# Where four pieces of bookkeeping stand in a two-block transformer kernel: two output projections' first weight pieces, a feed-forward norm, a key-value norm

## The reference

```python
def second_block(x, ...):
    for l in range(2):
        h = rmsnorm(x, g_attn[l])
        if l < 1: x = x + dsa_mixer(h, ...)           # sparse attention, then o @ w_o
        else:     x = x + nsa_mixer(h, kv_shared, ...) # three-branch attention, then o @ w_o
        x = x + sq_relu_mlp(rmsnorm(x, g_mlp[l]), w_up[l], w_down[l])
        if l == 0: kv_shared = shared_kv(x, ...)       # rmsnorm(x, g_kv) @ w_kv, then compressed blocks
    return rmsnorm(x, g_final)

def sq_relu_mlp(h, w_up, w_down):                      # 1024 -> 4096 -> 1024
    return jnp.square(jax.nn.relu(h @ w_up)) @ w_down
```

## Time and profile before

| | |
|---|---|
| median of 3 runs | 2052.91 us (2050.9 to 2053.53) |
| the profiled execution's own time | 2053.22 us |
| its span, first to last instruction | 2051.5 us |
| PE busy | 1959.5 us, 96% of the span, 9117 matmuls |
| DVE busy | 986.1 us, 48% |
| ACT busy | 662.8 us, 32% |
| POOL busy | 158.6 us, 8% |
| share of the chain that ended last | PE 86%, DVE 7%, ACT 2%, DMA 2% |
| mean granted PE clock | 0.978 of full speed |

### The profile page before, as it was taken

The page is one execution under the profiler, slowest core; times in us unless marked ns, Lnnn a source line. Parts: engine busy times, 40 slices in busy tenths (PEclk is TensorE's granted clock), DMA queues, the critical chain, the costliest instruction groups (busy, mean ns, idle before and its releaser), DMA issues.

```text
span 2051.5 us, 23968 instructions
## 1 busy us (share of the span) xinstructions
PE 1959.5 (96%) x9117; PEld 1357.6 (66%) x9117; DVE 986.1 (48%) x1865; ACT 662.8 (32%) x1238; POOL 158.6 (8%) x169
## 2 busy tenths in 40 slices
PE   7999899987999999988999999999999999999998
PEld 3478577573333334445788888878777778888886
DVE  6473645342121222674465455545256756455554
ACT  2572721141011112367332222232336633222222
POOL 1000000021111110213200000010000020000001
PEclk9999999997999999999999999999999999999999
DMA  9545143457999786111222322322540022232211
GB/s 323 196 125 205 43 160 128 186 175 280 417 381 354 274 338 226 42 42 42 83 82 82 122 84 82 123 82 82 172 153 2 1 83 82 82 124 82 83 40 41
DMA packets 104871, 292.55 MB, mean 143 GB/s; under 512 B 13445, under 2 KB 24403, under 8 KB 91712
## 3 DMA queue, kind: packets, MB, share of 16 engines
q1 hardware_dynamic: 92352, 266.60, 35.3%
q0 software_dynamic: 11408, 22.27, 3.5%
q10 hardware_dynamic: 1008, 2.29, 0.3%
HBM read 331.22 MB, written 24.69 MB: 173 GB/s over the span
## 4 chain that ended last, share of the span: by engine, by line
PE 86%; DVE 7%; ACT 2%; DMA 2%; issue 1%; POOL 1%; ACTq 0%; DVEq 0%; SPq 0%; POOLq 0%
PE bank L1402 17%; PE bank L1404 17%; PE bank L1403 17%; PE bank L1798 8%; PE bank L1319 5%; PE bank L1824 4%; PE bank L1361 3%; PE bank L1387 2%; PE bank L1373 2%; PE bank L1854 1%; PE bank L1606 1%; PE bank L1782 1%; DVE top L3268 1%; PE bank L1393 1%; DVE hT L3269 1%
## 5 line engine op out<-in xcount | busy, mean ns | idle before, releaser
L3159 DVE TENSOR_TENSOR weights_low<-weight_ring,weights_high 128x1024 fp32r<-128x1024 f32 x128 | 161.2, 1260 | 269.6 <-ACT weights_high L2282 269.6
L1404 PE MATMUL bank<-hidden_high,weights_low 128*128 128x512 f32 x704 | 274.5, 390 | 0.0
L1402 PE MATMUL bank<-hidden_high,weights_high 128*128 128x512 f32 x640 | 249.7, 390 | 6.0 <-DVE weights_low L2748 3.8
L1403 PE MATMUL bank<-hidden_low,weights_high 128*128 128x512 f32 x640 | 249.7, 390 | 0.0
L2282 ACT ACTIVATE weights_high<-weight_ring 128x1024 fp32r<-128x1024 f32 x128 | 135.6, 1060 | 324.2 <-PE bank L1404 324.2
L1402 PE MATMUL bank<-normed_high,weights_high 128*128 128x512 f32 x512 | 201.5, 394 | 3.9 <-DVE weights_low L3159 3.9
L1404 PE MATMUL bank<-normed_high,weights_low 128*128 128x512 f32 x512 | 200.6, 392 | 0.0
L1403 PE MATMUL bank<-normed_low,weights_high 128*128 128x512 f32 x512 | 200.5, 392 | 0.0
L1798 PE MATMUL bank<-weight_ring,arena 128*64 128x512 f32 x464 | 173.7, 604 | 4.4 <-issue 2.5
L1404 PEld LDWEIGHTS bank<-hidden_high,weights_low 128*128 128x128 f32 x704 | 132.6, 188 | 27.6
L1402 PEld LDWEIGHTS bank<-hidden_high,weights_high 128*128 128x128 f32 x640 | 120.5, 188 | 32.1 <-DVE weights_low L2748 7.0
(11 more groups left out here) (551 smaller groups left out, 3493.2 us busy)
## 6 DMA issues: line engine op xcount, KB each, us to landing
weight_ring<-in_w_up SPq DMA_DIRECT2D x16, 2048.0 KB, 8.7
weight_ring<-in_w_down SPq DMA_DIRECT2D x16, 2048.0 KB, 7.8
weight_ring<-in_w_gate SPq DMA_DIRECT2D x29, 1024.0 KB
weight_ring<-in_w_up SPq DMA_DIRECT2D x29, 1024.0 KB
weight_ring<-in_w_ada SPq DMA_DIRECT2D x12, 2048.0 KB, 12.6
weight_ring<-in_w_down SPq DMA_DIRECT2D x19, 1024.0 KB
hT<-in_w_down SPq DMA_DIRECT2D x19, 1024.0 KB
weight_ring<-in_w_in SPq DMA_DIRECT2D x7, 2048.0 KB, 14.5
```

Of the source, the lines that this page charges most:

```text
L1402: pe.matmul(dst, high, rhs_high, start=first, stop=False)
L1403: pe.matmul(dst, high, rhs_low, start=False, stop=False)
L1404: return pe.matmul(dst, low, rhs_high, start=False, stop=last)
L3159: dve.tensor_tensor(piece_half(w_lo, ch, q), piece_of(ch, q), piece_half(w_hi, ch, q).bitcast(F32), ALU.subtract).then_inc(s_wlo, 1)
```

## The change

Four things move; no instruction is added or taken away on any engine, and SP's and POOL's programs are the same.

1. Piece 0 of each output projection gets high and low buffers of its own (`first_sparse_out_*`, `first_last_out_*`) in memory that is free at that time, and is split inside the attention: for `d_o` by ACT in step 26 and by DVE in step 27, for `n_o` by ACT in step 24 and by DVE in step 25. In `n_o`, PE takes the eight tiles in another order (0, 4, 1, 5, 2, 3, 6, 7), and DVE splits four of them in steps of the attention.
2. In both feed-forward networks the sum of squares on PE stands behind the second up-piece (it was behind the first). ACT takes five tiles' `x_high` with only two squares among them, then the first weight piece, and the other six squares behind that; DVE splits two tiles of `normed_low` ahead of the first weight piece (it was four).
3. As the root comes later, the first up-block's results are read one piece later (`pieces_due`); the second up-block's third piece makes up for it with two.
4. The key-value norm's sums stand on PE behind all four first products; ACT's splits of pieces 2 and 3 stand among the squares, pieces 4 and 5 ahead of the root; DVE splits pieces 1 to 4 before the norm and builds the compressed blocks in two halves.

```diff
@@ list of groups
     for c in range(3):
         if c == 0:
             group("kvs_first", 2)
-            group("norm_kvs", 2)
         group(("kvs", c), 2 if c == 0 else 6)
         chunk(("kvs_w", c))
+        if c == 0:
+            group("norm_kvs", 2)
...
+        def pieces_due(ch, prev, q):
+            if prev is None:
+                return () if q < 3 else ((ch, 0),)
+            if ch is not None and ch[0] == "U" and isinstance(ch[2], int) and ch[2] == 1:
+                return {0: ((prev, 1),), 1: ((prev, 2),), 2: ((prev, 3), (ch, 0)), 3: ((ch, 1),)}[q]
+            return (two_before(ch, prev, q),)
...
@@ PE, mlp
-                        if prev is None and q == 0:
+                        if prev is None and q == 1:
                             g_free(pe, g + BANKS - 1)
                             pe.wait_ge(s_xsum, (KD - 1) * (2 * layer + 2))
...
@@ PE, shared keys and values
             for m in range(4):
-                if m == 2:
-                    g = G["norm_kvs"]
...
                 late_product(kvs_first(m), m, 0)
+            g = G["norm_kvs"]
+            begin(g)
+            pe.wait_ge(s_xsum, (KD - 1) * 3)
...
@@ ACT, mlp
-                        if prev is None and q < 2:
-                            for j in range(KD - 2) if q == 0 else ():
+                        if prev is None and q == 0:
+                            for j in range(5):
                                 x_high(j)
-                            act.wait_ge(mm_done, ch[4] - 1 + q)
-                            weights_high(ch, q)
-                            x_high(KD - 2 + q)
+                                if j < 2:
+                                    square(2 * layer + 1, j)
+                            act.wait_ge(mm_done, ch[4] - 1)
+                            weights_high(ch, 0)
+                            square(2 * layer + 1, 2)
+                            x_high(5)
+                            square(2 * layer + 1, 3)
+                            x_high(6)
+                            square(2 * layer + 1, 4)
+                            continue
+                        if prev is None and q == 1:
+                            act.wait_ge(mm_done, ch[4])
+                            weights_high(ch, 1)
+                            x_high(7)
+                            for j in range(5, KD):
+                                square(2 * layer + 1, j)
                             continue
...
@@ ACT, sparse attention and d_o
             def heads_up(s):
+                if s == ITEMS - 6:
+                    proj_weights_high("d_o", 0)
...
-            act.wait_ge(mm_done, done(G[("dsa", "V", ITEMS - 1)]))
-            proj_weights_high("d_o", 0)
             g_read(act, G[("o_up", H - 1)])
             operand_high(KD - 1, o_dsa[:, KD - 1, :])
+            act.wait_ge(mm_done, done(G[("dsa", "V", ITEMS - 1)]))
             proj_weights_high("d_o", 1)
...
@@ DVE, sparse attention, last attention
             def heads_low(s):
+                if s == ITEMS - 5:
+                    proj_weights_low("d_o", 0)
...
-            proj_weights_low("d_o", 0)
...
+            def first_output_low(s):
+                units = UNITS["nsa"]
+                if s == units - 7:
+                    proj_weights_low("n_o", 0)
+                if s in (units - 4, units - 3):
+                    j = output_tiles("n_o")[s - units + 4]
+                    operand_low("n_o", j, o_n[:, j, :])
...
```

More of the change, by code:

```diff
@@ L880, in late_used, with output_tiles @@
                 eng.wait_ge(mm_done, done(G[("kvs", p // 4)] + (5 if p % 4 == 3 else p % 4)))
+        def output_tiles(name):
+            return (0, 4, 1, 5, 2, 3, 6, 7) if name == "n_o" else range(KD)
         def late_low_x(n, k):
@@ L2001, in _ @@
             for m in range(4):
-                if m == 2:
-                    g = G["norm_kvs"]
-                    begin(g)
-                    pe.wait_ge(s_xsum, (KD - 1) * 3)
-                    pe.matmul(psum(g)[:, :], ones[:, :], x_sum[:, :], start=True, stop=True).then_inc(mm_done, 1)
-                    begin(g + 1)
-                    for t in range(NT):
-                        last = pe.matmul(psum(g + 1)[:, t:t + 1], x_sum[:, t * P:t * P + P], ones[:, 0:1], start=True,
-                                         stop=True)
-                    last.then_inc(mm_done, 1)
-                late_product(kvs_first(m), m, 0)
+                late_product(kvs_first(m), m, 0)
+            g = G["norm_kvs"]
+            begin(g)
+            pe.wait_ge(s_xsum, (KD - 1) * 3)
+            pe.matmul(psum(g)[:, :], ones[:, :], x_sum[:, :], start=True, stop=True).then_inc(mm_done, 1)
+            begin(g + 1)
+            for t in range(NT):
+                last = pe.matmul(psum(g + 1)[:, t:t + 1], x_sum[:, t * P:t * P + P], ones[:, 0:1], start=True,
+                                 stop=True)
+            last.then_inc(mm_done, 1)
             for n in (1, 2):
@@ L2570, in _ @@
             act.activation(kvs_scale[:, 0, :], kvs_scale[:, 0, :], ACT.Sqrt).then_inc(s_mstd, 1)
-            for p in range(3, 10):
+            for p in range(6, 10):
                 late_weights_high(p)
@@ L2634, in head_high @@
             def head_high(s):
+                if s == UNITS["nsa"] - 8:
+                    proj_weights_high("n_o", 0)
                 h = (s - 8) // NT
@@ L2641, in _ @@
             pair_attention("nsa", nsa_rest)
-            proj_weights_high("n_o", 0)
             head_high(UNITS["nsa"] + 4)
@@ L2694, in dsa_attention, with pair_attention @@
                     after(s)
-            def pair_attention(kind):
+            def pair_attention(kind, after=None):
                 base, scale, units = PAIR_BASE[kind], PAIR_SCALE[kind], UNITS[kind]
@@ L2735, in pair_attention @@
                                           ALU.add).then_inc(freed[g % BANKS], 1)
+                    if after is not None:
+                        after(s)
             def add_to_x(g, j, it=0, gate=None):
@@ L3182, in step @@
                         if prev is None and q == 0:
-                            for j in range(4):
+                            for j in range(2):
                                 x_low(j)
@@ L3186, in step @@
                             weights_low(ch, 0)
-                            for j in range(4, KD - 1):
+                            for j in range(2, 5):
                                 x_low(j)
@@ L3319, in _ @@
                 late_gained_low(0, j, col("g_kv_shared_2", j))
-            late_weights_low(1)
-            late_weights_low(2)
+            for p in range(1, 5):
+                late_weights_low(p)
             g = G["norm_kvs"]
@@ L3331, in _ @@
             dve.sem_inc(freed[(g + 1) % BANKS], 1)
+            late_weights_low(5)
             dve.wait_ge(s_mstd, 2)
@@ L3349, in _, with blocks @@
                 g_read(dve, kvs_first(m))
-            for n in range(2):
+            def blocks(n):
                 for gr in range(2):
@@ L3361, in _ @@
                     evac_scaled(G[("kvs", n + 1)] + m, (k_slc, k_win)[n][:, m, :])
+                    if n == 0:
+                        blocks(m)
                 if n == 0:
@@ L3413, in _ @@
             cmp_schedule(query, lambda i: None, cmp_probs, lambda i: None, lambda i: None)
-            pair_attention("nsa")
-            proj_weights_low("n_o", 0)
-            for j in range(KD):
+            def first_output_low(s):
[5 more added lines that the diff above has]
+                    operand_low("n_o", j, o_n[:, j, :])
+                if s in (units + 1, units + 2):
+                    j = output_tiles("n_o")[s - units + 1]
+                    if s == units + 1:
+                        dve.wait_ge(mm_done, done(G[("nsa", "S", units - 1)] + 1))
+                    operand_low("n_o", j, o_n[:, j, :])
+            pair_attention("nsa", first_output_low)
+            for j in output_tiles("n_o")[4:]:
                 operand_low("n_o", j, o_n[:, j, :])
```

55 lines of the change are left out of this document (32 added, 23 removed).

## The result

The changed kernel takes 2029.51 us (median of 4 runs, 2026.13 to 2034.28) against 2051.9 us before (4 runs, 2050.66 to 2053.53): ratio 0.9893, 95% interval 0.9882 to 0.9905, that is 22 us less, between 19.5 and 24.2. Timed a second time, beside other runs of the kernel before, the ratio is 0.9905 (0.9888 to 0.9921). The forecast was 19.0 us less, 2033.9 us; 2029.51 lies in the range, near its lower end.

A forecast was written before the change was run, and what follows sets the result against it. PE was taken as the bound, busy 96% of the span, so time returns only at its gaps and low clocks. Terms 5.1 + 2.2 + 8.5 + 3.2 = 19.0 us gave 2033.9 us, range 2029 to 2040 us.

The forecast's parts named there:

- `d_o`, 5.1 us: Start of `d_o`: 3.78 us gap and 1.7 us of low clock go, less 0.4 us cost: 5.1 us won.
- 0.4 us for the attention: Attention before `d_o`: the two splits cost 0.4 us, between 0 and 3.6 us; 0.5 to 1 us lost at first.
- the last head's `hidden_low`: Start of `d_o`: the next late input, at about 969 us; PE reaches that tile 4.8 us after 966.4 us.
- `n_o`, 2.2 us: Start of `n_o`: the 2.21 us gap goes and the attention's splits cost 0: 2.2 us won.
- Keys and values, 8.5 us: Shared keys and values: two PE gaps and the low clock go, 31.87 us become 23.4 us: 8.5 us won.
- Feed-forward networks, 1.6 us each: Both networks: the starting gap goes, but additions delay the second piece to 1023.1 from 1024.77 us: 1.6 us won each.
- one more addition and the second weight piece (1.27 + 1.15 us) to 1023.0 us: First network: a POOL addition goes ahead of DVE's second low half, which ends at 1023.0 us; PE waits some 2 us.
- no collision: Rival, networks: DVE wins the turns against POOL, each network wins 3.6 us; 2030 us in all, chance 0.17.
- The lower clock of the head: First network: clock 0.77 for 7.4 us, given no term because the second low half held PE up until then anyway.
- The clock did not fall: Rival: waits move and the clock falls again; networks win nothing or `d_o` keeps its low clock; 2037.3 or 2039 us, chance 0.14.
- The compressed weights moved along: Rival: the key-value gain is lost at the compressed weights if their transfer doesn't move along; 2042.4 us, chance 0.05.
- no up-piece waited for the one before: Rival "slower", networks: the later up-block read is never made up, every up-piece waits for the previous; 2060 us, chance 0.04.

The follow-up runs named there:

- experiment 6: The changed kernel with ACT's sixth square moved ahead of the last `normed_high` in each feed-forward network; 2037.06 us, ratio 0.994 against the kernel before.
- third run of experiment 7: DVE's and POOL's operations without the kernel, POOL idle before, additions released in some 2 ns steps, last DVE operation in plain, column or constant form; lost turns counted, no kernel time.
- first run of experiment 7: DVE's and POOL's operations without the kernel: six parts of 24 POOL additions beside uninterrupted DVE operations of several forms and widths; turns counted, no kernel time.

## Why the prediction was right, and where it was not

- **`d_o`, 5.1 us.** Right, in its steps too: 5.64 us by the stage, gap and low clock together, less the 0.28 us that the attention pays, is 5.4 us. The forecast took 0.4 us for the attention, 0.5 to 1 us lost at first and most of it regained; it lost 0.6 us and regained 0.3. Late next was the last head's `hidden_low`, as forecast.
- **`n_o`, 2.2 us.** Right for the execution it was read from: 2.43 us, and the attention pays nothing, as assumed. In two other profiles the lower clock followed the same gap, and the part is worth 4 us.
- **Keys and values, 8.5 us.** Right: 23.38 us against the forecast's 23.4, 8.47 us in the profile, 8.4 us timed alone.
- **Feed-forward networks, 1.6 us each.** This term was mis-sized: 3.2 us each in the changed kernel, 2.1 us where the turn is lost. The step that failed is "one more addition and the second weight piece (1.27 + 1.15 us) to 1023.0 us". Its premise was right, that the addition can start 0.4 us or more ahead of DVE's next operation (0.55 us); the conclusion, that it then goes first, was not. The rival "no collision", with a chance of 0.17, is what both profiles of the changed kernel show, for a reason that it didn't name. Where the addition did go first, PE waited 1.21 us, not 2, since DVE came 0.5 us earlier than by my count and PE 0.3 us later. The lower clock of the head, which the forecast made no term of its own, was worth 0.6 us of the 3.2 us; its argument that the second low half held PE up in any case covers only part of that clock's cost.
- **The sum.** The networks' surplus is 3.2 us, the other stages' 0.7 us: 22.95 us against 19.0 us. The first timed gain (19.5 to 24.2 us) holds 22.95 us and just leaves out 19.0 us; the second (16 to 23 us) holds both.
- **The skill's rule.** The Trainium skill, "SBUF — State Buffer", section "SBUF: two separate sides", which I let count in full, says that whichever starts first gets the shared ports for its whole instruction. That the loser waits in full agrees with the rows (2.31 us against 1.21 us). That the first to start gets them does not always, as the profile dates the starts: five of six plain splits went ahead of an addition 0.55 us older.
- **The rivals.** The clock did not fall, as no gap was left; experiment 6 shows that it can, behind 1.25 us. The compressed weights moved along (0.8 us of wait), and no up-piece waited for the one before.

## What to carry to other kernels

When an engine pair takes turns, don't decide a tie by who is ready first from a trace of another order: give the outcome both prices, and if the place is critical, put the other engine's start well inside an operation that you know is running (here one wait on ACT). Read stages between the busiest engine's own records, as a stage repeats there to 0.1 or 0.2 us where the clock stays at 1.00 (to 0.6 or 1.6 us where it falls in some executions), while timed runs of the same kernel scatter by up to 11 us. Where work is moved to fill a gap, look one neighbour further: one square exchanged with its neighbour cost 2.6 to 4.2 us a network.

## What the runs showed of the hardware that I had not expected

- In the third run of experiment 7 a POOL addition that began -9 to 72 ns behind DVE's change of operation lost the turn behind it in 42 of 144 cases when the next DVE operation was plain or had a constant (one of the 144 began earlier), in 0 of 48 when it read a scalar column. Of 18 later starts none was lost. In the first run, with another stream, none of 12 was lost. Why the column matters was not settled; in the first run of experiment 7 additions won against scaled operations issued up to 18 ns before them and against plain ones only if these came over 16 ns later, so a scaled operation seems to ask later.
- In the networks with the plain form DVE won five of six, more often than the 29% alone; what else weighs there is open.
- Equal gaps of PE were followed by the lower clock in one place or execution and not in another. In the second block's stages: gaps of 1.2 to 1.3 us ahead of a network's second piece in 1 of 7, of 1.96 us ahead of its first in 4 of 6, of 2.21 us at `n_o` in 2 of 3, of 3.78 us and more at `d_o` and the key-value norm in 6 of 6. It was worth 1.6 us behind 1.25 and 2.21 us, and 0.6 us behind 1.96 us, where PE had the second low half to wait for in any case.
